# Attention scores in two passes over stacked halves: a fused two-block transformer kernel on one core

## The reference

```
# neighbourhood attention (first block): 16 heads of 64, 512 queries, local window and 256 context keys
q = q * HEAD_DIM ** -0.5
s_loc = q . k over an 8 x 16 window + rpb bias ;  s_ctx = q . kc
p = softmax(concat(s_loc, s_ctx)) ;  o = p_loc . v + p_ctx . vc

# second block: 8 query heads of 64 over 2 key heads, queries and keys normed and rotated
s = einsum('bqkgd,btkd->bkgqt', q, k) * HEAD_DIM ** -0.5      # 768 keys: 256 context + 512 latent
p = softmax(s) ;  o = einsum('bkgqt,btkd->bqkgd', p, v)
# in its first layer the 256 context queries attend to the 256 context keys as well
```

## Time and profile before

| | |
|---|---|
| three timed runs | 2770.77, 2773.02, 2773.41 us |
| span of the profiled execution | 2770.2 us; the page gives no other time of that execution |
| TensorE matmuls | 2629.6 us busy (95%), 14006 |
| weight loads | 2200.8 us (79%) |
| VectorE | 1693.5 us (61%), 2670 |
| ScalarE | 951.6 us (34%), 1478 |
| GpSimd | 156.1 us (6%), 84 |
| DMA | 296.30 MB, mean 107 GB/s |

### The profile page before, as it was taken

One profiled execution on the slowest core, in us unless ns is written; L12 is line 12 of the kernel. 1 busy time (PEld: TensorE's weight loads), 2 busy tenths in 40 slices (PEclk: granted clock), 3 DMA queues, 4 the chain that ended last, 5 costly groups with the idle time before them and its releaser, 6 DMA issues. The chain is left out here.

```text
span 2770.2 us, 36208 instructions
## 1 busy us (share of the span) xinstructions
PE 2629.6 (95%) x14006; PEld 2200.8 (79%) x14006; DVE 1693.5 (61%) x2670; ACT 951.6 (34%) x1478; POOL 156.1 (6%) x84
## 2 busy tenths in 40 slices
PE   6999899999899999899899899999998999999999
PEld 3888688887778887788787788888887777888887
DVE  4887666666677988854567864444345456544433
ACT  3222444444332233433453322222223345323322
POOL 0000000000000000000461000000000036000000
PEclk8999999999999999999899999999999989999999
DMA  6243343433355625412002343334121200133233
GB/s 230 91 152 122 128 144 129 148 133 125 116 179 194 194 88 153 142 39 99 1 1 93 114 129 122 128 118 136 61 61 64 72 31 1 61 99 99 91 94 97
DMA packets 88539, 296.30 MB, mean 107 GB/s; under 512 B 10288, under 2 KB 13360, under 8 KB 87856
## 3 DMA queue, kind: packets, MB, share of 16 engines
q1 hardware_dynamic: 88368, 293.98, 32.5%
HBM read 291.85 MB, written 2.10 MB: 106 GB/s over the span
## 5 line engine op out<-in xcount | busy, mean ns | idle before, releaser
L903 PE MATMUL turns<-h_hi,w_hi 128*128 128x512 f32 (+1 forms) x2552 | 823.4, 366 | 41.1 <-DVE h_lo L1480 22.8
L903 PE MATMUL turns<-h_hi,w_lo 128*128 128x512 f32 (+1 forms) x2552 | 807.8, 359 | 0.0
L903 PE MATMUL turns<-h_lo,w_hi 128*128 128x512 f32 (+1 forms) x2552 | 802.4, 357 | 0.0
L903 PEld LDWEIGHTS turns<-h_hi,w_hi 128*128 128x128 f32 x2552 | 442.1, 192 | 135.4 <-DVE h_lo L1480 38.1
L1250 ACT ACTIVATE w_hi<-w_raw 128x1024 fp32r<-128x1024 f32 x300 | 316.0, 1054 | 528.5 <-PE turns L903 522.2
L903 PEld LDWEIGHTS turns<-h_hi,w_lo 128*128 128x128 f32 x2552 | 441.2, 192 | 69.6
L903 PEld LDWEIGHTS turns<-h_lo,w_hi 128*128 128x128 f32 x2552 | 439.5, 191 | 69.7 <-issue 1.0
L1477 DVE TENSOR_TENSOR w_lo<-w_raw,w_hi 128x1024 fp32r<-128x1024 f32 x300 | 366.5, 1222 | 98.4 <-ACT w_hi L1250 97.9
L853 POOL TENSOR_SCALAR tmp<-tmp,softmax_stats 128x768 f32<-128x768 f32 (+1 forms) x80 | 155.9, 1951 | 2192.0 <-DVE softmax_stats L1722 2191.9
L1480 DVE SCALAR_TENSOR_TENSOR x_lat<-turns,modulation,x_lat 128x512 f32<-128x512 f32 (+1 forms) x121 | 86.1, 711 | 292.0 <-PE turns L903 289.4
L903 PE MATMUL turns<-m_hi,w_lo 128*128 128x512 f32 (+1 forms) x768 | 237.2, 358 | 0.0
(11 more groups left out here) (239 smaller groups left out, 3154.9 us busy)
## 6 DMA issues: line engine op xcount, KB each, us to landing
w_raw<-in_wpack SPq DMA_DIRECT2D x300, 512.0 KB, 3.6
ada_raw<-in_adapack SPq DMA_DIRECT2D x176, 512.0 KB, 4.1
bias<-in_bias SPq DMA_DIRECT2D x64, 320.0 KB, 3.1
ada_first_a<-in_adapack SPq DMA_DIRECT2D x12, 512.0 KB, 8.7
x_lat<-in_xT SPq DMA_DIRECT2D x1, 2048.0 KB, 8.7
x_ctx<-in_ctxT SPq DMA_DIRECT2D x2, 1024.0 KB, 8.9
ada_first_b<-in_adapack SPq DMA_DIRECT2D x4, 512.0 KB, 14.7
cond_rows<-in_crow SPq DMA_DIRECT2D x4, 512.0 KB, 10.2
```

Of the source, the lines that this page charges most:

```text
L903: ins = pe.matmul(dst[:, lo:lo + sz], w, x[:, lo:lo + sz], start=first and n == 0, stop=last and n == 2)
```

## The change

The three passes become two. One factor is stacked: its rounded head in one half of the 128 rows and the rest of the same head in the other. The second factor holds the rounded head twice, in both halves. A 128-row matmul then gives hi·hi + lo·hi in one pass. The third product, hi·lo, stays a 64-row pass. In the neighbourhood keys are stacked (`KS`) and queries held twice (`QD`); in the second block queries are stacked (`SQ`) and keys held twice (`SK`). Roundings and rests are therefore written head by head, on 64 partitions each, some to the other half of the partitions. Some buffers move to other addresses (`WS`, `PVT`, `Ql`, `SKl`). No DMA is added.

```diff
+HEAD_ROWS = (slice(0, 64), slice(64, 128))
...
-        Qh, Ql = arena("q_hi", [P, 2, TX], F32R, 44 * K1), arena("q_lo", [P, 2, TX], F32R, 48 * K1)
-        Kh, Kl = arena("k_hi", [P, 2, TT], F32R, 52 * K1), arena("k_lo", [P, 2, TT], F32R, 58 * K1)
+        QD, Ql = arena("q_twice", [P, 2, 2, TX], F32R, 43 * K1), arena("q_lo", [P, 2, TX], F32R, 74 * K1)
+        KS = arena("k_stacked", [P, 2, 2, TT], F32R, 51 * K1)
...
-        SQh, SQl = arena("sq_hi", [P, 4, TT], F32R, 0), arena("sq_lo", [P, 4, TT], F32R, 12 * K1)
-        SKh, SKl = arena("sk_hi", [P, TT], F32R, 24 * K1), arena("sk_lo", [P, TT], F32R, 27 * K1)
+        SQ = [arena(f"sq_stacked{n}", [P, 4, TT], F32R, 12 * n * K1) for n in range(2)]
+        SK = [arena(f"sk_twice{n}", [P, TT], F32R, (24 + 3 * n) * K1) for n in range(2)]
+        SKl = arena("sk_lo", [P, TT], F32R, 74 * K1)
...
 # TensorE, scores (the context queries' loop changes in the same way)
-                        qh, ql, kh, kl = (x[r, s.pair % 2] for x in (Qh, Ql, Kh, Kl))
+                        p = s.pair % 2
+                        passes = (QD[:, s.half, p], KS[:, s.half, p]), (Ql[r, p], KS[r, s.half, p])
                     else:
-                        qh, ql, kh, kl = SQh[r, s.pair], SQl[r, s.pair], SKh[r], SKl[r]
-                    for n, (x, y) in enumerate(((qh, kh), (qh, kl), (ql, kh))):
+                        passes = (SQ[s.half][:, s.pair], SK[s.half]), (SQ[s.half][r, s.pair], SKl[r])
+                    for n, (x, y) in enumerate(passes):
...
 # ScalarE, rope
-                    give(act.activation(dst, (OWN[1] if s.own else T2)[:, 0:t], ACT.Copy))
+                    y = OWN[1] if s.own else T2
+                    for h, r in enumerate(HEAD_ROWS):
+                        if s.what == "sk":
+                            for twin in HEAD_ROWS:
+                                ins = act.activation(SK[h][twin, 0:t], y[r, 0:t], ACT.Copy)
+                        else:
+                            ins = act.activation(SQ[h][r, s.m, 0:t], y[r, 0:t], ACT.Copy)
+                    give(ins)
...
 # ScalarE, key and query units of the neighbourhood
-                            act.activation(dst[:, TX:TT], ps[:, TX:TT], ACT.Copy)
-                            give(act.activation(by_cols(dst[:, 0:TX]), by_rows(ps[:, 0:TX]), ACT.Copy))
+                            for h, r in enumerate(HEAD_ROWS):
+                                act.activation(KS[r, h, p, TX:TT], ps[r, TX:TT], ACT.Copy)
+                                ins = act.activation(by_cols(KS[r, h, p, 0:TX]), by_rows(ps[r, 0:TX]), ACT.Copy)
                         else:
                             chain(act.activation(by_cols(T1[:, 0:TX]), by_rows(ps[:, 0:TX]), ACT.Copy, scale=0.125))
-                            give(act.activation(dst[:, 0:TX], T1[:, 0:TX], ACT.Copy))
+                            for h, r in enumerate(HEAD_ROWS):
+                                for twin in HEAD_ROWS:
+                                    ins = act.activation(QD[twin, h, p, :], T1[r, 0:TX], ACT.Copy)
+                        give(ins)
...
 # VectorE, rope
-                    done(rest(lo, y[:, 0:t], hi))
+                    for h, r in enumerate(HEAD_ROWS):
+                        hi, lo = (SK[h][r, 0:t], SKl[r, 0:t]) if s.what == "sk" else (SQ[h][r, s.m, 0:t], SQ[h][HEAD_ROWS[1 - h], s.m, 0:t])
+                        ins = rest(lo, y[r, 0:t], hi)
+                    done(ins)
...
 # VectorE, key and query units of the neighbourhood
+                        for h, r in enumerate(HEAD_ROWS):
+                            if s.ev == "k":
+                                hi, lo = KS[r, h, p], KS[HEAD_ROWS[1 - h], h, p]
+                                rest(lo[:, TX:TT], ps[r, TX:TT], hi[:, TX:TT])
+                                ins = rest(by_cols(lo[:, 0:TX]), by_rows(ps[r, 0:TX]), by_cols(hi[:, 0:TX]))
+                            else:
+                                ins = rest(Ql[r, p, :], T1[r, 0:TX], QD[r, h, p])
+                        done(ins)
```

More of the change, by code:

```diff
@@ L683, in build_blocks @@
         ROPC, ROPS = arena("rope_cos", [P, TX], F32, 70 * K1), arena("rope_sin", [P, TX], F32, 72 * K1)
-        WS, BS = arena("w_spatial", [P, 512], F32, 74 * K1), arena("b_spatial", [P, 2, P], F32, 30 * K1)
+        WS, BS = arena("w_spatial", [P, 512], F32, 62 * K1), arena("b_spatial", [P, 2, P], F32, 30 * K1)
         DC = sb("dft_cos", [P, 4, TX], F32, h_at)
@@ L689, in build_blocks @@
         EX, PADDED = [T4, T2], [U, T3]
-        PVT = arena("pv_tmp", [P, 256], F32, 74 * K1)
+        PVT = arena("pv_tmp", [P, 256], F32, 63 * K1)
         adx_a, adx_b = arena("ada_first_a", [P, 12, D], F32, 0), sb("ada_first_b", [P, 4, D], F32, h_at)
@@ L1113, in _ @@
                             q = slice(TX + j * P, TX + j * P + P)
-                            for n, (x, y) in enumerate(((SQh, SKh), (SQh, SKl), (SQl, SKh))):
-                                ins = pe.matmul(SP_[:, s.st, j * TC:j * TC + TC], x[r, s.pair, q], y[r, TX:TT], start=n == 0, stop=n == 2)
+                            for n, (x, y) in enumerate(((SQ[s.half][:, s.pair], SK[s.half]), (SQ[s.half][r, s.pair], SKl[r]))):
+                                ins = pe.matmul(SP_[:, s.st, j * TC:j * TC + TC], x[:, q], y[:, TX:TT], start=n == 0, stop=n == 1)
                         ins.then_inc(score_mm[s.st], 1)
@@ L1125, in _ @@
                             k0, nl = min(c for c in NA_CHUNKS[s.qt]) * P, (s.nk - 2) * P
-                            pe.matmul(SP_[:, 0, at_l:at_l + nl], x[:, q], y[:, k0:k0 + nl], start=n == 0, stop=n == 2)
-                            ins = pe.matmul(SP_[:, 0, at_c:at_c + TC], x[:, q], y[:, TX:TT], start=n == 0, stop=n == 2)
+                            pe.matmul(SP_[:, 0, at_l:at_l + nl], x[:, q], y[:, k0:k0 + nl], start=n == 0, stop=n == 1)
+                            ins = pe.matmul(SP_[:, 0, at_c:at_c + TC], x[:, q], y[:, TX:TT], start=n == 0, stop=n == 1)
                         else:
                             for lo, sz in segs(TT):
-                                ins = pe.matmul(SP_[:, s.st, lo:lo + sz], x[:, q], y[:, lo:lo + sz], start=n == 0, stop=n == 2)
+                                ins = pe.matmul(SP_[:, s.st, lo:lo + sz], x[:, q], y[:, lo:lo + sz], start=n == 0, stop=n == 1)
                     ins.then_inc(score_mm[s.st], 1)
@@ L1419, in _ @@
                     elif s.ev in ("q", "k"):
-                        dst = (Qh if s.ev == "q" else Kh)[:, s.pair % 2]
+                        p = s.pair % 2
                         if s.ev == "k":
-                            act.activation(dst[:, TX:TT], ps[:, TX:TT], ACT.Copy)
-                            give(act.activation(by_cols(dst[:, 0:TX]), by_rows(ps[:, 0:TX]), ACT.Copy))
+                            for h, r in enumerate(HEAD_ROWS):
+                                act.activation(KS[r, h, p, TX:TT], ps[r, TX:TT], ACT.Copy)
+                                ins = act.activation(by_cols(KS[r, h, p, 0:TX]), by_rows(ps[r, 0:TX]), ACT.Copy)
                         else:
                             chain(act.activation(by_cols(T1[:, 0:TX]), by_rows(ps[:, 0:TX]), ACT.Copy, scale=0.125))
-                            give(act.activation(dst[:, 0:TX], T1[:, 0:TX], ACT.Copy))
+                            for h, r in enumerate(HEAD_ROWS):
+                                for twin in HEAD_ROWS:
+                                    ins = act.activation(QD[twin, h, p, :], T1[r, 0:TX], ACT.Copy)
+                        give(ins)
                     elif s.ev == "v" and s.pair is not None and s.layer is None:
@@ L1679, in _ @@
                     take()
-                    hi, lo = (SKh[:, 0:t], SKl[:, 0:t]) if s.what == "sk" else (SQh[:, s.m, 0:t], SQl[:, s.m, 0:t])
-                    done(rest(lo, y[:, 0:t], hi))
+                    for h, r in enumerate(HEAD_ROWS):
+                        hi, lo = (SK[h][r, 0:t], SKl[r, 0:t]) if s.what == "sk" else (SQ[h][r, s.m, 0:t], SQ[h][HEAD_ROWS[1 - h], s.m, 0:t])
+                        ins = rest(lo, y[r, 0:t], hi)
+                    done(ins)
                 elif s.kind == "vtrans":
@@ L1787, in _ @@
                         take()
-                        hi, lo = (Qh, Ql) if s.ev == "q" else (Kh, Kl)
                         p = s.pair % 2
[L1790 to L1794, removed]
+                        for h, r in enumerate(HEAD_ROWS):
[6 more added lines that the diff above has]
+                        done(ins)
                     elif s.ev == "cv":
```

## The result

The changed kernel takes 2823.53 us (median of four runs, 2817.49 to 2828.14) against 2771.89 us before: ratio 1.0184, 95% interval 1.017 to 1.0198. It is slower, as forecast, by 51.6 us where 27 were forecast. Its profiled execution, the fastest of the four, took 2817.49 us with a span of 2815.7, 45.5 us more than before; the other 6 us of the median are in no trace.

The account below looks back on a forecast made before the run. TensorE is busy 95% of the span, but its waits decide: neighbourhood +22.3, second block's keys and queries +10.3, clock +3.4, second attention -8.6, sum +27.4 on 2770.2 + 2.8, so 2800 us; range 2770 to 2818.

Parts of the forecast that it names:

- 1.3 us won back in seven pairs: Neighbourhood: of a pair's eight saved passes (2.1 us) only 1.3 us is really won, the rest precedes existing waits.
- 8.6 in the attention: Second attention: 4.3 us won in some 48 steady steps and 4.3 in six half-clock steps; -8.6 us.
- the loop over GpSimd: Second attention: a chain through GpSimd's scaling makes a four-step loop of 12.79 us, losing one 0.36 us pass, not four.
- The switch: Score steps: one entry to and exit from 64-row matmuls as before; 0 taken, 1.4 us at most in context steps.
- I take the neighbourhood's new gaps as harmless: Neighbourhood: new TensorE gaps cost no clock, since a gap of 2.0 us left the granted clock at 1.00.
- +1.7 a layer: Head of the second attention: half clock after the value transposes' 5.2 us gap, +3.4 us in all.
- The VectorE half hides behind the weight rest.: Second block's query roundings: VectorE's added rest costs nothing, as the weight rest waits for ScalarE.
- The query unit's stall, +2.0: Neighbourhood: four copies and two rests make the key unit wait for `q_lo`, +2.0 us a pair.
- no second stall: Neighbourhood: VectorE's work behind `q_lo` is 2.0 us late, but so are the transposes needing it; no further cost.
- Start-to-start paces: Roundings: added copies start 0.54 us apart for neighbourhood queries, 0.76 for second-block keys.
- Rival 3: Neighbourhood: each pair's 2.0 and 1.2 us gaps halve the clock for 4 us, 24 us more: 2824 us; chance 8%.
- Rival 1: Whole kernel: TensorE's columns decide, 2729 us, or about 2750 without a neighbourhood stall; chance 13%.

Follow-up runs that it names:

- e1: Changed kernel with its two passes, but the rounding of the kernel before (one copy, one rest over 128 partitions; scores not the reference's): 2755.82 us, ratio 0.9945.
- e2: Changed kernel with its second pass issued twice, so three passes again after the new rounding: 2841.56 us, ratio 1.025.
- e4: Changed kernel with the second pass over all 128 rows too, so no step changes its row count: 2814.62 us, ratio 1.015.
- e11: Changed kernel with six idle matmuls into the query's own PSUM bank, keeping TensorE at work in the gap before the key unit: 2822.14 us, ratio 1.0193.
- e10: Changed kernel with copies VectorE needs first, twins later, head-by-head hand-over, early releases of turn and score banks, 128-row second pass: 2765.04 us, ratio 0.9983.
- e7: Changed kernel; second block's score banks given back once VectorE has read them, value copy not waiting for the keys' rest: 2817.13 us, ratio 1.0163.
- e5: Changed kernel with the query's PSUM turn given back once ScalarE has copied it, not after VectorE's rest: 2826.77 us, ratio 1.0206.
- e8: Changed kernel with both early releases, second pass over 128 rows, rounding handed over head by head, old order of copies: 2785.27 us, ratio 1.0051.
- e9: Changed kernel with copies VectorE needs first, each head handed over by itself, twins and second halves later, no early release: 2807.62 us, ratio 1.0141.

## Why the prediction was wrong in size

The direction and the main mechanism held: the missing pass is cheap and the longer rounding dear. The waits came where they were named: 2.29 us before the key unit, 1.05 before the gate unit, 5.52 before the value transposes. What the passes win was sized right: the forecast has 1.3 us won back in seven pairs, 1.0 in the last and 8.6 in the attention, 18.7 us. e1's record is 19.0 us shorter than that of before, 13.3 of them in the neighbourhood; e2 puts the pass at 18 by the medians. The attention's two steps take 6.24 us, near the 6.2 named, and the loop over GpSimd is seen in the 14.0 us of its waits. The switch was rightly put at nothing against before: e4 shows that it costs 0.2 us a step, but the three-pass step paid it too. Of the miss of 18.1 us by the spans, 8.6 lie in the neighbourhood and 12.5 in the input stage of layer 0; the rest came out 3.0 better.

- *"I take the neighbourhood's new gaps as harmless" and "+1.7 a layer"* for the clock. This is the step that failed most. Over the whole span the mean granted clock fell from 0.972 to 0.966, 77.6 and 95.7 us short of full speed: 18 us more at most, since a low clock costs nothing where TensorE stands, where 3.4 were forecast. All else made 27, where 24.0 were. Layer 0's input stage ran 62 us at 0.76, at most 14.9 us lost, against 3.2 before (46 us at 0.93): +11.7 by the rows. That, with waits of 3.5 us more for the value transposes and 1.3 to 1.5 for each of three head norms, is the stage's +19.7. In the neighbourhood e11 shows 5.2, and the four slower pairs of the changed kernel 6. My row for "harmless" was one window behind one gap of 2.0 us. The trace of before also had others, where the neighbourhood begins, at the wait of 1.59 us of the earlier trace rows:

```profile
300.00:304.00 4.00, 2.19 (x12) 1.52 (x12) 3.10 (x6) 1.50 (x3) 0.00 (x0) 1.00 0.00 0
304.00:308.00 4.00, 2.41 (x7) 1.82 (x6) 1.92 (x2) 2.47 (x5) 0.00 (x0) 0.53 0.99 308
308.00:312.00 4.00, 4.00 (x13) 3.13 (x12) 2.58 (x5) 1.06 (x1) 0.00 (x0) 0.61 0.75 293
```

  In the input stage the clock was not changed by itself in any run: e10 takes the gaps away and the clock comes back with them.
- *"The VectorE half hides behind the weight rest."* It doesn't. The head norm writes a bank that the rotation's step gives back when its last rest is made, so the second rest is on TensorE's path. The waits became 1.83 to 1.93 us for VectorE, where 0.51 + 0.76 = 1.27 for ScalarE were forecast. (With the bank given back early, e7, ScalarE's own wait is 1.63.)
- *The query unit's stall, +2.0.* The stall came (2.29), but it was not a matter of the turn. e5 freed the turn and won nothing; e8 and e9 changed how ScalarE hands the heads to VectorE and won 22 and 17 us. Behind the stall both queues stand in order: VectorE 3.35 us at the rest, and the weight's rest and the next step's minimum behind the four copies. I named that queue and took its delay as absorbed by the stall ("no second stall"); with the stall gone in e5, the same delay came back as waits on the softmax.
- *Start-to-start paces.* I took 0.54 us a query copy and 0.76 a key copy, the full-width overlap. On alternating halves there is none: 2.56 us for four and not 2.25, 3.41 and not 3.13, rests 1.39 and not 1.30. A pair without a drop of the clock takes 3.75 us more than before and not 3.0; with the drops the mean is +4.78.

Rival 3 had the clock. That its 2824 us is the measured time is luck: it put 24 us into the neighbourhood, where the runs show 5 to 6, and nothing more than the forecast's 1.7 into layer 0's input stage, where the rows show up to 11.7. Rival 1's 2750 without a stall in the neighbourhood is near what e1 shows (2755.82) with the rounding of before.

## What to carry to other kernels

Before buying TensorE columns with work on another engine, ask what stands in order behind that work on its queue; freeing the buffer that the trace names may only move the wait. Hand pieces over one by one as the next engine needs them. Where evictions wait behind them, put the copies needed later behind the evictions, together with an early release. Count a new gap of two microseconds with the half clock that may come after it, and look for every such gap in the trace before; one window at full clock does not clear the rest.

## What the runs showed of the hardware

- Instructions that change to the other 64 partitions do not overlap their predecessor: ScalarE's four query copies take 4 x 0.64 us, where full-width ones start 0.54 after one of 0.63; VectorE's two rests 2 x 0.69. Two key copies within one half still overlap (0.38 us long, the next 0.28 later). The Trainium skill (VectorE: DVE Perf Modes, Two Vector instructions with no wait between them) says that an instruction whose input or output starts in another quadrant than the last one's is held until that has finished. The trace agrees for VectorE, and shows the same on ScalarE.
- 64-row matmuls between 128-row ones cost 0.2 us a visit (28.0 us in 136 steps, e4). The Trainium skill (TensorEngine Tiling (Array Packing), Key Properties) says that a change of tiling mode drains TensorE. The runs agree in the cost; the draining itself is in no row.
- A second pass over all 128 rows, with the other head's rests in the idle half, runs at the 64-row pace and saves the switch (e4: matmuls of 256 columns start 0.12 us apart, through both passes).
